# Two of the four moves of each unit's turned probabilities go from SyncE to ScalarE

## The chip, the cores and the metric

One core of a Trainium2 chip runs the whole program. The metric is the device time of one execution in microseconds (us); lower is better. Two executions of the kernel before took 2779.14 and 2780.52 us, median 2779.83.

## What is computed

One layer of a sequence model on x of 2048 tokens by 2048 features, all in float32. The normalised input is multiplied with one wide weight matrix; its columns feed three head groups, each with its own gate; one output matrix follows. Cut to what matters here:

```python
h = rmsnorm(x, ln_gain)
q_a, k_a, v_a, g_a, b_c, c_c, x_c, g_c, q_m, g_m = split(h @ w_in)
# A: 16 query heads, 2 key heads of 64; a chunk of 64 queries sees 128 keys; bias, one sink a head
p = softmax(concat([q_a k_a^T / 8 + bias, sink]))[..., :-1];  o_a = p @ v_a
# M: 4 heads of 128 over 256 memory tokens
p = softmax(q_m k_m^T / sqrt(128));                           o_m = p @ v_m
o_c = b_c * causal_dwconv3(c_c * x_c)
out = x + concat([silu(g_a) o_a, silu(g_c) o_c, silu(g_m) o_m]) @ w_out
```

## The kernel before

The program is written out by hand for each engine; every engine runs its own instructions strictly in the order of the text, and waits for others on semaphores. PE is the matmul engine, DVE VectorE, ACT ScalarE, POOL GpSimd, SP SyncE.

**Slots.** All work is set against slots. A slot is one load of 512 KB of weights: SP loads it (`weights`, L540), ACT rounds its two halves into w_hi (`high`, L765, two instructions), POOL computes w_lo = raw - w_hi (L655), and PE multiplies three products for each pair of parts (hi hi, hi lo, lo hi), 24 products of 512 columns a slot (L1729 to L1731). ACT and POOL prepare slot s + 2 in iteration s. After 16 slots for the memory tokens come four groups of 512 tokens with 52 slots each (blocks KV, QA0, QA1, QM, C, X, B), and then 224 slots for gates and output (L1801 to L1805), in which no attention is left.

**Units.** In each group 24 units of attention run beside the slots: A units (one chunk of queries and one key head) in the odd slots 17 to 47, M units (memory attention) in the even slots 34 to 48. So there is one unit in two slots at first, and one in each slot from 33 on. For a unit in slot s:

- PE computes the scores behind the matmuls of slot s (`scores`, L1872 or L1866).
- DVE adds the bias (L1421), finds the maxima (L1433, or L1411 for M), and ACT computes the exponentials (`softmax_exp`, four instructions L984 for A, two L975 for M, with sums).
- DVE divides (L1449) and transposes blocks of 32 by 32 into blocks_t (`turn_probs`, L1458); this raises the semaphore turned.
- Four DMAs of 64 KB (`move_probs`, L548) bring the four groups of 32 rows of blocks_t to probs_t, all of them issued by SP. SP does this before the weights of slot s + 6; its wait for turned stands ahead of them.
- In iteration s + 2, for an A unit, ACT writes pt_hi from probs_t (`probs_high`, L995) when all four moves have landed, and DVE pt_lo (L1381). DVE does this before it touches the next A unit's scores.
- In iteration s + 3 PE multiplies with the values (`values`, L1900 and L1901, or L1891 for M), ACT copies the result (`attention_out`, L1010 for A, L1005 for M), and for A DVE adds the second half (`attention_sum`, L1393), which comes ahead of DVE's softmax in that iteration. PE's next `values` waits for it.

**ACT's order in iteration s** is: parts of the next group's input (L891), `evacuate`, `high` for slot s + 2, `attention_out`, `probs_high`, `softmax_exp`, then the issues of larger transfers where the tables name the slot: t_store and t_load (weight sums), rows_store, h_store (L808), x_load (L776), and x_square and x_scale on xt (L795, L801), and h_load (L814). An ACT DMA that waits on a semaphore stands in the same order as ACT's arithmetic.

Of the kernel before, what the change touches and what calls it, by code (L numbers as in the profile page):

```python
# [80 lines left out]
UNITS = len(UNIT)  # L81
# [4 lines left out]
SCORES_AT = {s: u for u, s in enumerate(UNIT_SLOTS)}  # L86
# [100 lines left out]
def program(nc, x, mem, ln_gain, w_in, q_norm_a, k_norm_a, sinks, conv_w, mem_ln_gain, w_mem_kv,  # L187
# [5 lines left out]
    with ctx:  # L193
        def sb(name, shape, dt=F32):
            return ctx.enter_context(nc.sbuf_tensor(name, shape, dt))
# [4 lines left out]
        def sem(name):  # L200
            return ctx.enter_context(nc.semaphore(name))
# [48 lines left out]
        blocks_t = sb("blocks_t", [P, 2, 4, P])  # L250
        probs_t = sb("probs_t", [P, 2, 4, P])
# [103 lines left out]
        turned = sem("turned")  # L355
        moved = [sem(f"moved{i}") for i in range(2)]
# [178 lines left out]
        def _(sp):  # L535
# [7 lines left out]
            def move_probs(g, u):  # L543


                sp.wait_ge(turned, g * UNITS + u + 3)
                for i in range(4):
                    sp.dma_start(probs_t[:, u % 2, i, :], blocks_t[32 * i:32 * i + 32, u % 2, :, :]  # L548
                                 ).then_inc(moved[u % 2], 16)

# [71 lines left out]
            for j in range(OUT_SLOTS):  # L622
                r, i, s = j // PAIR_SLOTS, j % PAIR_SLOTS // PRODUCT_SLOTS, j % PRODUCT_SLOTS
# [124 lines left out]
        def _(act):  # L748
# [95 lines left out]
            def low_load(kq):  # L844

                act.wait_ge(half_used, 2 * OUT_BASE - 16 + 4 * kq + 4)
                h_fetch(1, kq, tiles4(x_low, kq), low_in[kq])
# [39 lines left out]
            def h_high(g, k):  # L887

                act.wait_ge(h_in[k // 4], 16 * g + 16)
                act.wait_ge(half_used, 2 * (MEM_SLOTS + (g + 1) * GROUP_SLOTS - SB_SLOTS) + k + 1)  # L890
                nc.scalar.activation(in_32s(h_hi[:, k, :]), x_row(h_buffer(k // 4), k),  # L891
                                     ACT.Copy).then_inc(x_hi, 1)
# [25 lines left out]
            def t_store(g, n):  # L918

                act.wait_ge(t_step, 4 * (SB_SLOTS * g + n + 1))  # L920
                act.dma_start(w_sums[g, :, P * n:P * n + P, :].rearrange("s p c -> p s c"),
                              stage[:, :, :]).then_inc(t_stored, 16)
# [39 lines left out]
            def conv_latest_tap(g):  # L962

                for b in range(4):
                    act.wait_ge(bank_free[b], g * USES + MEM_USES + 6)
                    nc.scalar.activation(ungated[:, 8 + b, :], early[:, 8 + b, :], ACT.Copy,
                                         scale=taps[:, 2, b:b + 1]).then_inc(conv_first, 1)

            def softmax_exp(g, u):
                U = g * UNITS + u  # L970
                if UNIT[u][0] == "M":
                    act.wait_ge(shifted, U + 1)
                    act.wait_ge(turned, U + 1)
                    for h in range(2):
                        e = nc.scalar.activation(probs[:, u % 2, 256 * h:256 * h + 256],  # L975
                                                 ps_t[:, 256 * h:256 * h + 256], ACT.Exp,
                                                 bias=shift[:, h:h + 1],
                                                 accum_out=total[:, h:h + 1])
                else:
                    act.wait_ge(sink_ready, g * LOCAL_UNITS + LOCAL[u] + 1)  # L980
                    nc.scalar.activation(sink_exp[:, :], sink_in[:, :], ACT.Exp)
                    for p in range(4):
                        s = probs[:, u % 2, P * p:P * p + P]
                        e = nc.scalar.activation(s, s, ACT.Exp, bias=shift[:, p:p + 1],  # L984
                                                 accum_out=total[:, p:p + 1])
                e.then_inc(exped, 1)

            def probs_high(g, u):
                U = g * UNITS + u
                act.wait_ge(moved[u % 2], g * 768 + (u // 2) * 64 + 64)  # L990
                if LOCAL[u]:
                    act.wait_ge(valued, g * UNITS + LOCAL.index(LOCAL[u] - 1) + 2)
                else:
                    act.wait_ge(valued, g * UNITS + 1)
                nc.scalar.activation(pt_hi[:, :], probs_t[:, u % 2, :, :].rearrange("p a q -> p (a q)"),  # L995
                                     ACT.Copy).then_inc(pt_high, 1)
# [59 lines left out]
            def a_high(j, h):  # L1056

                r, i, s = j // PAIR_SLOTS, j % PAIR_SLOTS // PRODUCT_SLOTS, j % PRODUCT_SLOTS
                name = PRODUCTS[i][0]
                kq = (2 * s + h) // 4  # L1060
                if name in ("S3", "S1", "S4"):
                    act.wait_ge(s_made, sums_to(j) - 1 + h)
                elif name == "S2":
                    act.wait_ge(s2_step, 16 * (r // 2) + 4 * s + h + 3)
                elif gating(r):
                    if name == "A22":
                        act.wait_ge(low_in[2 + kq], 16 * (r // 4) + 16)
                    else:
                        act.wait_ge(top_in[kq + 2 * (name == "A12")], 16 * (r // 4) + 16)
                elif name == "A11":  # L1070
                    act.wait_ge(mixed, 32 * (r // 4) + 16)
                else:
                    act.wait_ge(mixed, 32 * (r // 4) + 32)
                if j >= 2:
                    act.wait_ge(half_used, 2 * (OUT_BASE + j - 2) + h + 1)
                else:
                    act.wait_ge(t_stored, 16 * SB_SLOTS * GROUPS)
                if j in (2, 3):
                    act.wait_ge(o_ready, GROUPS * UNITS + 1)
                nc.scalar.activation(in_32s(a_parts(j, h)[0]), a_source(j, h),  # L1080
                                     ACT.Copy).then_inc(a_hi_ready, 1)

            for g in range(GROUPS):
                base = g * GROUP_SLOTS + MEM_SLOTS
                last = g == GROUPS - 1
                for s in range(GROUP_SLOTS):
                    if last and s >= GROUP_SLOTS - 2:
                        for h in range(2):
                            a_high(s - GROUP_SLOTS + 2, h)
                    if g:  # L1090
                        for k in H_SPLIT_NEXT.get(s, ()):
                            h_high(g - 1, k)
                    if not last:
                        for k in H_SPLIT_AT.get(s, ()):
                            h_high(g, k)
                    if s in LAST_SLOT:
                        evacuate(*LAST_SLOT[s], g, base + s + 1)
                    if s == CONV_FIRST_AT:
                        conv_latest_tap(g)
                    high((s + 2) % 4, base + s + 2)  # L1100
                    if s in VALUES_AT:
                        attention_out(g, VALUES_AT[s])
                    if s in SPLIT_AT:
                        probs_high(g, SPLIT_AT[s])
                    if s in SCORES_AT:
                        softmax_exp(g, SCORES_AT[s])
                    if s in T_STORE_AT:
                        t_store(g, T_STORE_AT[s])
                    if s in T_LOAD_AT:
                        t_load(g, T_LOAD_AT[s])  # L1110
                    if s in ROWS_STORE_AT:
                        rows_store(g, ROWS_STORE_AT[s])
                    if g:
                        for quarter in ROWS_STORE_NEXT.get(s, ()):
                            rows_store(g - 1, quarter)
                    if s in H_STORE_AT:
                        h_store(g, H_STORE_AT[s])
                    if s in X_LOAD_AT:
                        x_load(g, X_LOAD_AT[s])
                    if s in X_SQUARE_AT:  # L1120
                        x_square(g, X_SQUARE_AT[s])
                    if s in X_SCALE_AT:
                        x_scale_of(g, X_SCALE_AT[s])
                    if last:
                        for kq in TOP_LOAD_AT.get(s, ()):
                            top_load(kq)
                        if s in LOW_LOAD_AT:
                            low_load(LOW_LOAD_AT[s])
                    else:
                        for kq in H_LOAD_AT.get(s, ()):  # L1130
                            h_load(g, kq)
# [871 lines left out]
```

## Time and profile before

| | |
|---|---|
| median of 2 executions | 2779.83 us |
| profiled execution | 2779.99 us, its span 2778.2 us |
| PE, DVE, ACT, POOL busy | 95%, 67%, 45%, 63% of the span |
| granted clock of PE over the span | 0.98 |
| moves (64 KB each) | 384, median 2.2 us from issue to landing |
| four groups of tokens | up to about 1500 us; gates and output behind |

A busy share of PE of 95% is a mean over stages; matmuls are pipelined, and what a stage is bounded by is read from its waits. SPq and ACTq are the issues of DMAs by SP and ACT, which don't count as busy. A line of the timeline gives start, duration, engine, line, operation and tiles, and in brackets how long the engine was idle before it and what ended that.

### The profile page before, as it was taken

To read this page: it belongs to the slowest core of one execution; us is meant where nothing else is said; L and a number is where in the kernel's file an instruction comes from. 1 tells how busy PE (TensorE), PEld (TensorE's weight loads), DVE (VectorE), ACT (ScalarE), POOL (GpSimd) and SP (SyncE) were. 2 spreads that over 40 slices of the span, in tenths; PEclk is the share of its full clock that TensorE was granted. 3 is DMA by queue.
4 is the path that set the end of the run, shared out by engine and by line. 5 is a ranking of instruction groups with operands and counts; after the bars stand their busy time and mean duration, and the time that the engine had idled before them with its cause. 6 is when DMAs were issued, how large, how long until landed. Compare 5 with 4: busy or idle time off the path is not lost.

```text
span 2778.2 us, 33924 instructions
## 1 busy us (share of the span) xinstructions
PE 2631.3 (95%) x12092; PEld 2151.6 (77%) x12092; DVE 1855.8 (67%) x2324; ACT 1258.1 (45%) x2660; POOL 1741.5 (63%) x1190
## 2 busy tenths in 40 slices
PE   7999899998999989999899999999999999999999
PEld 6877678776777768777687778777888878877887
DVE  4347576376764666646666786887677786797667
ACT  6344353454443545434453445443444444443443
POOL 6577444775547755387554567766667567666766
PEclk9999999999999999999999999999999999999999
DMA  8566756666556666656668633247445633324444
GB/s 252 157 202 188 232 151 200 226 201 203 171 183 225 198 183 197 203 186 217 179 203 258 222 92 96 87 141 223 152 144 167 219 91 99 91 91 144 159 129 144
DMA packets 329613, 479.70 MB, mean 173 GB/s; under 512 B 19094, under 2 KB 135908, under 8 KB 326884
## 3 DMA queue, kind: packets, MB, share of 16 engines
q1 hardware_dynamic: 191412, 278.28, 33.7%
q10 hardware_dynamic: 138032, 199.25, 21.6%
q8 instruction: 97, 1.59, 0.2%
q14 instruction: 72, 0.59, 0.1%
HBM read 355.03 MB, written 84.67 MB: 158 GB/s over the span
## 4 chain that ended last, share of the span: by engine, by line
PE 52%; DVE 20%; issue 8%; ACT 7%; POOL 5%; DMA 4%; SPq 3%; ACTq 1%; DVEq 0%; POOLq 0%
PE acc L1729 6%; PE acc L1730 6%; PE acc L1731 6%; PE acc L1801 5%; PE acc L1803 5%; PE acc L1805 5%; POOL w_lo L655 3%; DMA probs_t<-blocks_t 3%; DVE a_lo L1592 3%; SPq L548 2%; DVE blocks_t L1458 2%; ACT probs L984 2%; PE ps_s L1801 2%; DVE s_sum L1587 2%; PE ps_o L1801 1%
## 5 line engine op out<-in xcount | busy, mean ns | idle before, releaser
L655 POOL TENSOR_TENSOR w_lo<-raw,w_hi 128x512 fp32r<-128x512 f32 x896 | 1307.8, 1475 | 949.1 <-ACT w_hi L765 947.2
L765 ACT ACTIVATE w_hi<-raw 128x512 fp32r<-128x512 f32 x896 | 544.5, 627 | 808.7 <-PE acc L1731 267.0
L1729 PE MATMUL acc<-w_hi,h_hi 128*128 128x512 f32 (+1 forms) x1024 | 377.9, 369 | 12.6 <-POOL w_lo L655 12.5
L1731 PE MATMUL acc<-w_hi,h_lo 128*128 128x512 f32 (+1 forms) x1024 | 372.9, 364 | 0.0
L1730 PE MATMUL acc<-w_lo,h_hi 128*128 128x512 f32 (+1 forms) x1024 | 372.7, 364 | 0.0
L1729 PE MATMUL acc<-h_hi,w_hi 128*128 128x512 f32 x768 | 319.6, 416 | 7.8 <-DVE early L1507 5.7
L1730 PE MATMUL acc<-h_lo,w_hi 128*128 128x512 f32 x768 | 306.1, 399 | 0.0
L1731 PE MATMUL acc<-h_hi,w_lo 128*128 128x512 f32 x768 | 305.6, 398 | 0.0
L1592 DVE TENSOR_TENSOR a_lo<-s_sum,a_hi 128x512 fp32r<-128x512 f32 x192 | 216.9, 1162 | 33.8 <-ACT a_hi L1080 29.5
L1729 PEld LDWEIGHTS acc<-w_hi,h_hi 128*128 128x128 f32 x1024 | 194.1, 190 | 52.8 <-POOL w_lo L655 21.2
L1731 PEld LDWEIGHTS acc<-w_hi,h_lo 128*128 128x128 f32 x1024 | 193.9, 189 | 30.8
L1730 PEld LDWEIGHTS acc<-w_lo,h_hi 128*128 128x128 f32 x1024 | 194.2, 190 | 28.8
L1080 ACT ACTIVATE a_hi<-s_sum 128x512 fp32r<-128x512 f32 x192 | 117.7, 629 | 172.1 <-DVE s_sum L1587 167.1
L1729 PEld LDWEIGHTS acc<-h_hi,w_hi 128*128 128x128 f32 x768 | 149.6, 195 | 45.6 <-POOL w_lo L655 9.0
L1801 PE MATMUL acc<-a_hi,w_hi 128*128 128x512 f32 x448 | 176.3, 394 | 7.8 <-issue 4.2
L1801 PE MATMUL acc<-w_hi,a_hi 128*128 128x512 f32 x448 | 175.0, 391 | 4.6 <-DVE a_lo L1592 4.4
L1803 PE MATMUL acc<-a_lo,w_hi 128*128 128x512 f32 x448 | 175.6, 392 | 0.0
L1805 PE MATMUL acc<-a_hi,w_lo 128*128 128x512 f32 x448 | 175.5, 392 | 0.0
L1803 PE MATMUL acc<-w_lo,a_hi 128*128 128x512 f32 x448 | 174.3, 389 | 0.0
L1805 PE MATMUL acc<-w_hi,a_lo 128*128 128x512 f32 x448 | 174.3, 389 | 0.0
L1731 PEld LDWEIGHTS acc<-h_hi,w_lo 128*128 128x128 f32 x768 | 148.2, 193 | 33.1
L1730 PEld LDWEIGHTS acc<-h_lo,w_hi 128*128 128x128 f32 x768 | 149.0, 194 | 30.6
(278 smaller groups left out, 5456.0 us busy)
## 6 DMA issues: line engine op xcount, KB each, us to landing
raw<-in_w_in SPq DMA_DIRECT2D x256, 512.0 KB, 4.3
raw<-w_sums SPq DMA_DIRECT2D x128, 512.0 KB, 3.7
w_sums<-stage ACTq DMA_DIRECT2D x32, 1024.0 KB, 5.4
probs_t<-blocks_t SPq DMA_DIRECT2D x384, 64.0 KB, 2.2
raw<-in_w_out SPq DMA_DIRECT2D x48, 512.0 KB, 3.6
early<-h_rows ACTq DMA_DIRECT2D x17, 1024.0 KB, 7.8
xt<-in_x ACTq DMA_DIRECT2D x16, 1024.0 KB, 8.6
stage<-in_w_in ACTq DMA_DIRECT2D x32, 512.0 KB, 4.7
```

The costliest lines, as they stand in the source:

```text
L548: sp.dma_start(probs_t[:, u % 2, i, :], blocks_t[32 * i:32 * i + 32, u % 2, :, :]).then_inc(moved[u % 2], 16)
L655: nc.gpsimd.tensor_tensor(w_lo[:, at, :], raw[:, slot_mod, HALF * half:HALF * half + HALF], w_hi[:, at, :].bitcast(F32), ALU.subtract).the ...
L765: nc.scalar.activation(w_hi[:, 2 * (slot_mod % 2) + half, :], raw[:, slot_mod, HALF * half:HALF * half + HALF], ACT.Copy).then_inc(hi_read ...
L984: e = nc.scalar.activation(s, s, ACT.Exp, bias=shift[:, p:p + 1], accum_out=total[:, p:p + 1])
L1080: nc.scalar.activation(in_32s(a_parts(j, h)[0]), a_source(j, h), ACT.Copy).then_inc(a_hi_ready, 1)
L1592: nc.vector.tensor_tensor(in_32s(lo), a_source(j, h), in_32s(hi.bitcast(F32)), ALU.subtract).then_inc(a_lo_ready, 1)
L1729: nc.tensor.matmul(dst, st[0], mv[0], start=first, stop=False)
L1730: nc.tensor.matmul(dst, st[0], mv[1], start=False, stop=False)
L1731: return nc.tensor.matmul(dst, st[1], mv[0], start=False, stop=last)
L1801: nc.tensor.matmul(banks[t][:, :], st[0], mv[0], start=first, stop=False, skip_group_check=True)
L1803: nc.tensor.matmul(banks[t][:, :], st[0], mv[1], start=False, stop=False, skip_group_check=True)
L1805: last = nc.tensor.matmul(banks[t][:, :], st[1], mv[0], start=False, stop=s == 3 and h == 1, skip_group_check=True)
```

## The change

SP issues moves 0 and 1 of each unit, at its place of before. ACT issues moves 2 and 3, directly behind the unit's exponentials in `softmax_exp`, ahead of all transfers and of x_square and x_scale of that iteration; before them it waits for turned, which DVE raises with the unit's transpose. The semaphores that the readers wait for are the same, with the same counts. It does so for all 96 units. Nothing is computed otherwise.

```diff
--- before.py
+++ after.py
@@ -544,7 +544,7 @@
 
 
                 sp.wait_ge(turned, g * UNITS + u + 3)
-                for i in range(4):
+                for i in range(2):
                     sp.dma_start(probs_t[:, u % 2, i, :], blocks_t[32 * i:32 * i + 32, u % 2, :, :]
                                  ).then_inc(moved[u % 2], 16)
 
@@ -985,6 +985,13 @@
                                                  accum_out=total[:, p:p + 1])
                 e.then_inc(exped, 1)
 
+            def move_probs(g, u):
+
+                act.wait_ge(turned, g * UNITS + u + 3)
+                for i in range(2, 4):
+                    act.dma_start(probs_t[:, u % 2, i, :], blocks_t[32 * i:32 * i + 32, u % 2, :, :]
+                                  ).then_inc(moved[u % 2], 16)
+
             def probs_high(g, u):
                 U = g * UNITS + u
                 act.wait_ge(moved[u % 2], g * 768 + (u // 2) * 64 + 64)
@@ -1104,6 +1111,7 @@
                         probs_high(g, SPLIT_AT[s])
                     if s in SCORES_AT:
                         softmax_exp(g, SCORES_AT[s])
+                        move_probs(g, SCORES_AT[s])
                     if s in T_STORE_AT:
                         t_store(g, T_STORE_AT[s])
                     if s in T_LOAD_AT:
```

## Rows read from the trace of the kernel before

**Rows 1.** The page: busy time by engine, and the chain that ended last

```profile
PE 2631.3 (95%) x12092; PEld 2151.6 (77%) x12092; DVE 1855.8 (67%) x2324; ACT 1258.1 (45%) x2660; POOL 1741.5 (63%) x1190
...
PE 52%; DVE 20%; issue 8%; ACT 7%; POOL 5%; DMA 4%; SPq 3%; ACTq 1%; DVEq 0%; POOLq 0%
```

**Rows 2.** Busy time by stretch: start:end, length, engines with instructions, clock, DMA, GB/s

```profile
640.00:800.00 160.00, 143.42 (x686) 117.00 (x687) 106.47 (x183) 73.06 (x214) 72.73 (x52) 0.95 0.64 189
```

**Rows 3.** Waits of the matmul engine, 430 to 780 us: total, times, longest

```profile
PE ps_o L1900 <- DVE pt_lo L1381: 14.0, 5, 5.4
PE ps_o L1891 <- DVE ungated L1393: 3.9, 3, 2.5
```

**Rows 4.** Timeline of ACT, 706 to 719 us: start, duration, instruction, idle before

```profile
706.81 0.39 ACT L984 ACTIVATE probs<-probs,shift 128x128 f32<-128x128 f32 x1
...
708.36 1.14 ACT L765 ACTIVATE w_hi<-raw 128x512 fp32r<-128x512 f32 x2
...
709.52 0.77 ACT L1010 ACTIVATE ungated<-ps_o 64x256 f32<-64x256 f32 x2
...
713.12 1.15 ACT L765 ACTIVATE w_hi<-raw 128x512 fp32r<-128x512 f32 x2
...
714.16 0.38 ACT L1005 ACTIVATE ungated<-ps_o 128x256 f32<-128x256 f32 x1
...
714.82 0.63 ACT L995 ACTIVATE pt_hi<-probs_t 128x512 fp32r<-128x512 f32 x1 [0.28 <-DMA probs_t<-blocks_t]
...
718.75 0.39 ACT L984 ACTIVATE probs<-probs,shift 128x128 f32<-128x128 f32 x1
```

**Rows 5.** Timeline of DVE, the same stretch

```profile
709.62 1.10 DVE L1458 STREAM_TRANSPOSE blocks_t<-probs 128x512 f32<-128x512 f32 x1
710.64 0.81 DVE L1393 SCALAR_TENSOR_TENSOR ungated<-ps_o,ungated 64x256 f32<-64x256 f32 x2
...
715.16 1.09 DVE L1458 STREAM_TRANSPOSE blocks_t<-probs 128x512 f32<-128x512 f32 x1
716.18 0.65 DVE L1381 TENSOR_TENSOR pt_lo<-probs_t,pt_hi 128x512 fp32r<-128x512 f32 x1
```

**Rows 6.** The moves' line: issue min/median/max ns, first and last start; landing

```profile
L548 SPq DMA_DIRECT2D probs_t<-blocks_t x384: 544/603/2455, 188.1 to 1487.7; - x192
...
DMA to landing us min/median/max: 2.1/2.2/6.8
```

**Rows 7.** Waits of the whole span, all engines

```profile
ACT pt_hi L995 <- DMA probs_t<-blocks_t: 98.9, 35, 7.7
...
DVE ungated L1393 <- ACT ungated L1010: 16.0, 11, 2.3
```

**Rows 8.** Timeline of ACT, 589 to 595 us: issues behind a wait

```profile
589.75 3.32 ACTq L808 DMA_DIRECT2D h_rows<-early  x4
...
593.83 1.15 ACT L765 ACTIVATE w_hi<-raw 128x512 fp32r<-128x512 f32 x2 [6.85 <-issue]
```

**Rows 9.** Timeline of ACT, slot 35: the second h_load's issue

```profile
676.09 3.48 ACTq L814 DMA_DIRECT2D xt<-h_rows  x1
```

**Rows 10.** The chain of waits, 676 to 690 us: the landing of slot 35's moves

```profile
681.28 6.79 DMA probs_t<-blocks_t
```

**Rows 11.** Timelines of ACT and DVE at slots 43 and 44

```profile
734.40 2.55 ACT L966 ACTIVATE ungated<-early,vecs 128x512 f32<-128x512 f32 x4
...
738.82 0.85 DVE L1393 SCALAR_TENSOR_TENSOR ungated<-ps_o,ungated 64x256 f32<-64x256 f32 x2 [2.06 <-ACT ungated L1010]
```

**Rows 12.** Timeline of DVE behind slot 45's transpose

```profile
751.45 2.98 DVE L1291 TENSOR_TENSOR h_lo<-early,h_hi 128x512 fp32r<-128x512 f32 x2
```

**Rows 13.** Timeline of ACT at slots 28 and 29

```profile
615.71 2.01 ACT L801 ACTIVATE xt<-xt,x_scale 128x2048 f32<-128x2048 f32 x1
...
620.24 0.63 ACT L995 ACTIVATE pt_hi<-probs_t 128x512 fp32r<-128x512 f32 x1 [1.48 <-DMA probs_t<-blocks_t]
```

**Rows 14.** Timeline of SP at slot 37's place: move_queries

```profile
644.09 8.61 SPq L555 DMA_DIRECT2D early<-ungated  x4
```

## The prediction

> **What bounds the kernel now.** I read the page's busy line and the chain that ended last [rows 1]. The matmul engine is busy 95% of the span and makes 52% of the chain; DVE has 20%, ACT 7%, transfers 4%, SP's issue 3%. So the end is mostly the matmuls' own time, but not everywhere. The table by stretch [rows 2] shows 640 to 800 us, the second half of group 1's softmax work, with the matmul row 143.4 us busy of 160 at a granted clock of 0.95. The moves' issues are spread from 188.1 to 1487.7 us [rows 6], so the change can act only before 1500.
>
> Then the waits of the matmul engine in group 1 (430 to 780 us) [rows 3]: 14.0 us for pt_lo and 3.9 us for the sum L1393, the two largest there. So in this stage the softmax loop and the matmuls are nearly level: when the loop is late, the matmuls wait for it in values().
>
> Last the loop itself, at the pair of units (slots 39 and 40) where it runs without disturbance. One A and one M unit take from A's first exponential at 706.81 to the next A's at 718.75, 11.9 us. ACT [rows 4]: **two w_hi at 708.36, in the instant in which A's exponentials end, attention_out at 709.52**, two w_hi behind M's exponentials at 713.12, M's output at 714.16, pt_hi at 714.82. DVE [rows 5]: A's transpose 709.62 to 710.72, **the sum L1393 directly behind it at 710.64**, M's transpose 715.16 to 716.25, **pt_lo directly behind it at 716.18**. DVE does not pause except for ACT's exponentials. What the reader is to see: while DVE divides and transposes (2.3 us for A: from the exponentials' end, 0.09 behind 708.36, to 710.72), ACT does the work that DVE wants next. Matmuls: one slot is 24 products; two slots with their scores and values fill about the same 12 us.
>
> **What the change removes.** SP issues two moves instead of four. Four take 2.49 us, 0.60 each, and the last lands 2.2 us after its issue [rows 6]. Two on each of two queues: both pairs are issued in 1.2 us, so the last lands 1.2 us earlier. That is worth something only where pt_hi waits for the landing: 98.9 us in 35 of 64 units [rows 7], so at most 35 x 1.2 = 42 us over the kernel. SP's weights behind it also go out 1.2 us earlier; what they wait for is POOL's low parts, and the matmuls' large waits are elsewhere [rows 3]: nothing.
>
> The Trainium skill ("DMA: Bandwidth & Descriptors", section "Issuing engines are not separate DMA queues") says that starting transfers from several engines saves only the sequencer's time to start them, and calls it small. By that rule alone the sum would be the gain of this paragraph and no more; it says nothing of what the new issuer leaves undone.
>
> **What it adds.** ACT's queue is in order. Behind each of 96 units' exponentials it will stand until the transpose is done (2.3 us in the A unit of [rows 4, 5]) and then issues two moves. ACT's issue of a like transfer is not in the trace; the nearest are its four h_store issues, 3.32 us [rows 8], 0.83 each, with contention, and SP's 0.60 each. I take 1.2 us for two, and 1.7 as the other end. The same rows are the proof that a wait ahead of an issue holds ACT: h_store's issues wait for DVE's x_gain until 589.75, and the w_hi behind them comes only at 593.83, after 6.85 us in which ACT does nothing. So per unit ACT gives away 2.3 + 1.2 = 3.5 us in which it now works; all of it on the end would be 96 x 3.5 = 336 us.
>
> Replay of the pair, counted from each transpose's end (T):
> A unit: 1.2 issue + 1.14 w_hi + 0.77 attention_out = 3.1 us, then the sum, which now starts at T - 0.08. **+3.2 us.**
> M unit: 1.2 + 1.15 + 0.38 + 0.63 = 3.35 us to pt_hi's end, then pt_lo, which now starts at T. **+3.3 us.** The pt_hi there is that of the A unit before, whose moves have landed by then.
> Together +6.5 on 11.9 us, and nothing covers it, as DVE has no pause and the matmuls are level with it.
>
> The other seven pairs of a group, by the same counting:
> Slot 33: the second half also waits for block C's four copies, now behind M's transpose: +3.2 + 4.5, say +8.
> Slot 35: h_load's issues, 3.48 us for the second alone, lie beside the exponentials and DVE's division now [rows 9] and come behind the moves then: A's sum +4.9, M's half +2.6, +7.5. Here the moves themselves gain: unit 35's took 6.79 us to land behind that 2 MB [rows 10] and will be ahead of it; but ACT would by then be the later one.
> Slots 37 and 41: M's half is partly covered (a slow landing, DVE's additions for block X): +4.4 each.
> Slot 43: ACT's 2.55 us of L966 already makes DVE's sum wait 2.06 us [rows 11]; behind the transpose it makes it wait 5.7: +3.6, and +3.3 for M: +7.
> Slots 45 and 47: DVE has its own work behind each transpose, 2.98 us of h_lo behind A's [rows 12] and the convolution behind M's. That hides most: A +1.9, M +0.3, +2.2 each.
> Sum 8 + 7.5 + 4.4 + 6.5 + 4.4 + 7 + 2.2 + 2.2 = 42 us a group.
>
> Slots 17 to 31 (A units only, two slots apart): ACT has longer until pt_hi. At 615.71 it does 2.01 us of x_scale, w_hi at 617.62, and waits 1.48 us for the landing before pt_hi at 620.24 [rows 13]. Then: T at 616.12 + 1.2 + 1.14 + 0.77 + 2.0 + 1.14 = 622.4, +2.1. Without x_scale about 0. At slot 25 ACT has an x_square and the copies of a whole block between the exponentials and pt_hi, with no pause, so all 3.5 us count. At slot 31 SP's moves stand behind move_queries, 8.61 us of issue beside ACT's h_store, until 652.74, 6.5 us after T [rows 14]; with h_store held back that issue runs faster: -3. The eight: 0.3 + 1.5 + 0.1 + 1.2 + 3.5 + 2.1 + 1 - 3 = +6.7, say +6 a group.
>
> So +48 a group, x4 = 192; the last group has one top_load instead of two at slot 35, -3. **+189 us.** The profiled execution took 2779.99 us (span 2778.2), the median of the runs shown is 2779.83, so they are one number here. 2780 + 189 = 2969; I say **2967**. The clock: in the stretch in which the matmuls wait for the loop it is 0.95 [rows 2]. More waits will bring more time at the lower level, but beside a late loop a slower matmul costs nothing; zero, and some tens of us at the upper end.
>
> **Rivals.**
> A, gain: ACT's delayed work is short enough, and the earlier landing decides. The place is pt_hi L995, the price -1.2 us in each of 35 units, 2738 us. For it: the 98.9 us of rows 7. It decides where ACT's work between transpose and pt_hi is under the landing's 2.2 us. Against it: that work is 1.14 + 0.77 + 1.14 us or more [rows 13]. 5%.
> B, hidden: ACT is busy only 45% [rows 1], so 3.5 us find room there. 2780. Against: its pauses are those in which DVE computes for it, and what ACT does before them is what DVE waits for. 8%.
> C, half: of the two delays of a pair only one reaches the next pair, because the matmuls' slack of a slot or DVE's other work takes the other. 3.3 x 8 x 4 = 106 us, 2886. 15%.
> D, all of it: every unit pays 3.5 us, and the half clock comes more often when matmuls wait at each unit, 3116 us or near it. 7%.
> My own case: 65%.
>
> **The numbers.** A measurement of this kernel tells 2% (56 us) from no change. Faster by over 2% needs 2724, below even rival A, so only 2% for more gain than I can find. Within 2%: the rest of A and B, 11%. Slower: C, D and my case, 87%. The range: my terms are uncertain by a third (issue at 1.7 us for two adds 96 x 0.5 = 48 at most, covered halves take away as much), 2905 to 3040; to take in C it starts at 2865. **2865 to 3045.**
>
> **What the profile after would show.** ACT's time from the end of an A unit's exponentials to the next w_hi grows from nothing to about 3.5 us. The waits "DVE ungated L1393 <- ACT ungated L1010" (16.0 us in 11 now [rows 7]) grow to some 100 us or more, and pt_lo's wait for pt_hi grows; pt_hi's wait for the moves falls from 98.9 us to under 40. The matmul engine's waits for pt_lo and L1393 grow from 18 to about 60 us a group. The distance between A units' exponentials in slots 39 and 41 is 18 us. From 1500 us on (counted back from the end) nothing changes. I would be wrong if w_hi came right behind the exponentials, if the sum came at the transpose's end, or if the matmuls' waits of a group did not grow.

## The result and the profile after

The changed kernel took 3071.52 us (two executions, 3071.40 and 3071.63) against 2779.83: ratio 1.105 (95% interval 1.103 to 1.108), **292 us slower**. The direction and the main mechanism (ACT is held until the transpose is done) were those of the prediction; the size was not: 187 us were forecast, and the time lies above the range, which ended at 3045.

The page of the changed kernel, its lines that answer to [rows 1]:

```profile
PE 2724.4 (89%) x12092; PEld 2217.0 (72%) x12092; DVE 1865.5 (61%) x2324; ACT 1259.1 (41%) x2660; POOL 1709.5 (56%) x1190
...
PE 43%; DVE 22%; ACT 12%; issue 9%; ACTq 8%; POOL 5%; DMA 1%; SPq 0%; DVEq 0%; POOLq 0%
```

The matmul engine's share of the chain went from 52% to 43%; ACT's from 7% to 12%, and ACT's queue, where the issues are, from 1% to 8%.

The busy time by stretch of group 1, slots 17 to 33 and slots 33 to 48 (columns as in [rows 2]):

```profile
612.80:752.50 139.70, 114.24 (x485) 89.32 (x484) 80.37 (x121) 56.63 (x143) 71.89 (x49) 0.91 0.55 165
752.50:917.00 164.50, 119.38 (x506) 95.04 (x505) 76.53 (x131) 57.05 (x173) 54.36 (x42) 0.86 0.45 130
```

Before, these stretches took 119.7 and 112.4 us (from the first exponential of slot 17's unit to that of slot 33's, and on to slot 48's); now they take 139.7 and 164.5. Busy times of DVE and ACT stay what they were (76.5 and 57.1 us in the second stretch), the matmul engine is busy for only 119.4 of the 164.5 us, and its granted clock falls from 0.99 to 0.86.

The waits of the matmul engine in group 1 (answer to [rows 3]; 502 to 923 us, which lies to group 1's units as 430 to 780 us does before):

```profile
PE ps_o L1899 <- DVE ungated L1401: 29.4, 7, 5.4
PE acc L1737 <- POOL w_lo L655: 16.7, 9, 4.4
PE acc L1737 <- ACT ungated L959: 10.3, 1, 10.3
PE ps_o L1908 <- DVE pt_lo L1389: 8.5, 7, 3.2
```

The 14.0 and 3.9 us for pt_lo and the sum are 8.5 and 29.4 now, and 16.7 us for POOL's low parts and 10.3 us for ACT's copies of block C have come beside them.

ACT at slots 39 and 40 (answer to [rows 4]):

```profile
820.33 0.39 ACT L984 ACTIVATE probs<-probs,shift 128x128 f32<-128x128 f32 x1
...
824.70 1.47 ACTq L992 DMA_DIRECT2D probs_t<-blocks_t  x2
...
826.27 1.15 ACT L765 ACTIVATE w_hi<-raw 128x512 fp32r<-128x512 f32 x2 [4.30 <-PE acc L1739]
...
827.44 0.77 ACT L1017 ACTIVATE ungated<-ps_o 64x256 f32<-64x256 f32 x2
...
833.75 1.47 ACTq L992 DMA_DIRECT2D probs_t<-blocks_t  x2
835.32 1.16 ACT L765 ACTIVATE w_hi<-raw 128x512 fp32r<-128x512 f32 x2 [4.45 <-issue]
836.38 0.37 ACT L1012 ACTIVATE ungated<-ps_o 128x256 f32<-128x256 f32 x1
836.64 0.62 ACT L1002 ACTIVATE pt_hi<-probs_t 128x512 fp32r<-128x512 f32 x1
...
841.04 0.39 ACT L984 ACTIVATE probs<-probs,shift 128x128 f32<-128x128 f32 x1
```

and DVE there (answer to [rows 5]):

```profile
823.59 1.08 DVE L1466 STREAM_TRANSPOSE blocks_t<-probs 128x512 f32<-128x512 f32 x1
828.25 0.85 DVE L1401 SCALAR_TENSOR_TENSOR ungated<-ps_o,ungated 64x256 f32<-64x256 f32 x2 [3.58 <-ACT ungated L1017]
...
832.62 1.10 DVE L1466 STREAM_TRANSPOSE blocks_t<-probs 128x512 f32<-128x512 f32 x1
837.29 1.82 DVE L1389 TENSOR_TENSOR pt_lo<-probs_t,pt_hi 128x512 fp32r<-128x512 f32 x1 [3.58 <-ACT pt_hi L1002]
```

The A unit's transpose ends at 824.67. ACT's two moves are issued from 824.70 to 826.17, w_hi follows, attention_out begins at 827.44, and the sum L1401 begins at 828.25, 3.58 us behind the transpose where it was directly behind it. With M's transpose the same: it ends at 833.72, pt_hi begins at 836.64 and pt_lo at 837.29. The next A unit's exponentials start at 841.04: 20.7 us for the pair, before 11.9.

The waits of the whole span (answer to [rows 7]), and ACT's new line, its issue times and the time to landing (answer to [rows 6]):

```profile
ACT w_hi L765 <- issue: 284.9, 62, 8.4
DVE ungated L1401 <- ACT ungated L1017: 225.4, 60, 8.1
DVE pt_lo L1389 <- ACT pt_hi L1002: 197.0, 56, 7.7
```

```profile
L992 ACTq DMA_DIRECT2D probs_t<-blocks_t x192: 551/633/1514, 187.2 to 1776.6; - x192
...
DMA to landing us min/median/max: 2.1/2.4/6.1
```

The sum's waits for ACT grew from 16.0 to 225.4 us, pt_lo's waits for pt_hi from 154.3 to 197.0. No wait of pt_hi for the moves, 98.9 us before, is left: the moves land in time now, but ACT itself comes later than they do. Behind the last unit nothing changed: from the first exponential of slot 48 in the last group to the end are 1296 us before and 1297 after.

### The profile page after: what moved, and what is told of

Read it like the earlier page. It is cut to its first block, busy times and chain, and to the rows that moved or that the text cites. A ratio compares the mean times of both kernels' runs of the same rounds, so it can differ in the third digit from the quotient of the medians.

```text
span 3069.8 us, 33924 instructions
## 1 busy us (share of the span) xinstructions
PE 2724.4 (89%) x12092; PEld 2217.0 (72%) x12092; DVE 1865.5 (61%) x2324; ACT 1259.1 (41%) x2660; POOL 1709.5 (56%) x1190
## 4 chain that ended last, share of the span: by engine, by line
PE 43%; DVE 22%; ACT 12%; issue 9%; ACTq 8%; POOL 5%; DMA 1%; SPq 0%; DVEq 0%; POOLq 0%
PE acc L1809 5%; PE acc L1811 5%; PE acc L1813 5%; PE acc L1737 4%; ACTq L992 4%; PE acc L1738 4%; PE acc L1739 4%; ACT w_hi L765 3%; DVE blocks_t L1466 3%; POOL w_lo L655 3%; ACT probs L984 2%; DVE probs L1457 2%; DVE a_lo L1600 2%; PE ps_s L1809 1%; DVE probs L1429 1%
## 5 line engine op out<-in xcount | busy, mean ns | idle before, releaser
L655 POOL TENSOR_TENSOR w_lo<-raw,w_hi 128x512 fp32r<-128x512 f32 x896 | 1282.1, 1447 | 1255.3 <-ACT w_hi L765 1253.4
L1737 PE MATMUL acc<-h_hi,w_hi 128*128 128x512 f32 x768 | 341.0, 444 | 92.7 <-ACT ungated L959 39.7
L1738 PE MATMUL acc<-w_lo,h_hi 128*128 128x512 f32 (+1 forms) x1024 | 379.4, 371 | 0.0
L1738 PE MATMUL acc<-h_lo,w_hi 128*128 128x512 f32 x768 | 323.5, 421 | 0.0
L1739 PE MATMUL acc<-h_hi,w_lo 128*128 128x512 f32 x768 | 320.6, 417 | 0.0
L1737 PEld LDWEIGHTS acc<-h_hi,w_hi 128*128 128x128 f32 x768 | 161.3, 210 | 138.9 <-issue 69.6
L1389 DVE TENSOR_TENSOR pt_lo<-probs_t,pt_hi 128x512 fp32r<-128x512 f32 x64 | 77.3, 1208 | 197.0 <-ACT pt_hi L1002 197.0
L1401 DVE SCALAR_TENSOR_TENSOR ungated<-ps_o,ungated 64x256 f32<-64x256 f32 x128 | 53.4, 417 | 226.4 <-ACT ungated L1017 225.4
L1739 PEld LDWEIGHTS acc<-h_hi,w_lo 128*128 128x128 f32 x768 | 158.7, 207 | 37.5
L1738 PEld LDWEIGHTS acc<-h_lo,w_hi 128*128 128x128 f32 x768 | 161.0, 210 | 33.8
```

What stands on the lines that cost most here:

```text
L655: nc.gpsimd.tensor_tensor(w_lo[:, at, :], raw[:, slot_mod, HALF * half:HALF * half + HALF], w_hi[:, at, :].bitcast(F32), ALU.subtract).the ...
L1737: nc.tensor.matmul(dst, st[0], mv[0], start=first, stop=False)
L1738: nc.tensor.matmul(dst, st[0], mv[1], start=False, stop=False)
L1739: return nc.tensor.matmul(dst, st[1], mv[0], start=False, stop=last)
```

## The experiments

All run beside the kernel before, whose median beside them was 2777 to 2779 us. Gains and losses are against that median. The edits are shortened. Those of experiments 2, 10, 14 and 15 start from the kernel before, the others are shown against the changed kernel. H, Q and W are three theories of the loss, explained in the first expectation. "A group" is one of the four groups of tokens; the stretch of slots 17 to 33 took 120 us before and 139 in the changed kernel, that of 33 to 48 111 (105 in the last group) and 165 (160).

**1. The wait alone.**

```diff
 def move_probs(g, u):            # ACT; SP issues all four
     act.wait_ge(turned, g * UNITS + u + 3)
-    for i in range(2, 4): act.dma_start(...)
```

> ACT waits for turned behind each unit's exponentials but issues nothing; SP issues all four moves as before. Theory H (ACT is held: its w_hi, attention_out and pt_hi come only behind the transpose, and DVE's loop waits for them): in the tight pair the sum starts 1.14 + 0.77 = 1.9 us behind the transpose instead of 3.6 and pt_lo 2.2 instead of 3.6, so a bit over half of the loss of 292 us: 2920 to 2960 us. Theory Q (issuing transfers on ACT, or two queues beside each other, is what costs): 2780. Theory W (the loss is w_hi that comes too late for POOL and the matmuls): w_hi comes right behind the transpose, 1.5 us earlier than in the changed kernel; about 2900.

2952.23 us, ratio 1.063 (1.061 to 1.065): +175, 60% of the loss with not one move issued by ACT. The sum waited for ACT:

```profile
DVE ungated L1398 <- ACT ungated L1014: 130.5, 53, 5.4
```

Theory Q cannot have this.

**2. The issues alone.**

```diff
+    for i in range(2, 4):        # no wait ahead; source a constant tile, target a spare array
+        act.dma_start(spare[...], mem_k[32 * i:32 * i + 32, 0:2, :]).then_inc(spared, 16)
```

> The kernel before, and ACT issues two transfers of 64 KB behind each unit's exponentials with no wait ahead of them (from a constant tile in SBUF to a spare array in HBM, results unused); SP issues all four moves. 192 more transfers than before. H: ACT's sequencer hands them out while the exponentials run, so 1.5 us of issue are mostly covered: 2780 to 2830. Q: most of the loss, over 3000.

2786.19 us, ratio 1.0033 (1.0021 to 1.0045): +9. Issues cost little where nothing holds them: ACT's queue hands them out while the exponentials run. In slot 39 they start at 707.72 and 708.09 us, the exponentials run from 707.80 to 709.34, and w_hi starts there. Two issues behind the wait cost 292 - 175 = 117 us, 1.2 us for each of 96 units. These are not quite the same issues: here the target is memory, and they took 0.33 and 0.44 us. Experiment 4 makes the comparison with the very same moves.

**3. All four by ACT.**

```diff
-    for i in range(2, 4):        # ACT
+    for i in range(4):           # ACT; SP none
```

> ACT issues all four moves behind its wait, SP none. Two more issues of 0.74 us each stand ahead of w_hi: H: each of 96 units pays another 1.5 us on the loop, +140, and the last move lands 1.2 to 1.5 us later than in the changed kernel but still ahead of pt_hi: 3190 to 3240 us. Q: the queues no longer work beside each other, no change or a gain against 3072. W: +0 to +100.

3161.11 us, ratio 1.138 (1.136 to 1.140): 90 us more than with two, 0.93 us a unit where I expected 1.5, and below the range of 3190 to 3240. Two more issues delay w_hi by 1.1 us (it starts 2.70 us behind the transpose's end in slot 39, with two moves 1.60), so the third and fourth take 0.53 each. The sum:

```profile
DVE ungated L1401 <- ACT ungated L1017: 284.7, 60, 8.2
```

**4. The same moves, one iteration later.**

```diff
 probs_high(g, SPLIT_AT[s])
+move_probs(g, SCORES_AT[s - 1])  # ACT: the unit of the slot before
 softmax_exp(g, SCORES_AT[s])
-move_probs(g, SCORES_AT[s])
```

> The same two moves of each unit by ACT, with the same wait, but one iteration later: behind that iteration's w_hi, attention_out and pt_hi and ahead of its exponentials. By then the transpose is done and ACT would be idle, waiting for DVE's shift. H: the whole loss goes, and the earlier landing is left: 2740 to 2785 us. Q: the same issues and queues, so about 3070. W: w_hi is on time, so also 2780; it differs from H in that nothing is gained or lost at DVE's sum.

2789.66 us, ratio 1.0040 (1.0025 to 1.0055). Same queues, same 192 issues, same wait: 280 of the 292 us are gone. It is 5 us above the range of 2740 to 2785, since the expected gain did not come. The sum and pt_hi:

```profile
DVE ungated L1402 <- ACT ungated L1017: 12.9, 11, 2.1
...
ACT pt_hi L1002 <- DMA probs_t<-blocks_t: 10.6, 9, 3.2
```

pt_hi's wait for the moves fell from 98.9 to 10.6 us and yet the kernel is not faster: slots 17 to 33 took 124 us, 4 more than before. There the issues, 1.5 us, stand ahead of the next iteration's x_scale and w_hi, and thereby of pt_hi.

**5 and 6. Only the A units, only the M units.**

```diff
-for i in range(2):               # SP
+for i in range(2 if UNIT[u][0] == "A" else 4):    # e5; "M" in e6; ACT likewise
```

> Only the 64 A units are as in the changed kernel; SP issues all four moves of the 32 M units. H (ACT is held, and the delays of A and M units add, each at its own place, A's at the sum L1393, M's at pt_lo): the tight pair takes 11.9 + 3.6 = 15.5 us, slots 17 to 33 stay at 139 us as in the changed kernel, 33 to 48 at 138; a group loses 46 of 72 us: 2960 us. Theory C (of two delays in a pair only one reaches the next pair): near 3070.

> Only the 32 M units are as in the changed kernel. H: slots 17 to 33 as before (120 us), the tight pair 11.9 + 3.6 + 1.2 (pt_lo beside POOL's w_lo) = 16.7 us, 33 to 48 at 140 us; a group loses 28 us: 2890 us. The losses of this run and of the run with A units alone add up to the 292 us of the changed kernel. C: this run alone near 3070 in slots 33 to 48, and the two sum to much more than the whole.

A units alone: 2962.67 us, +184 (ratio 1.066, 1.064 to 1.068). M units alone: 2872.96, +95 (1.034, 1.032 to 1.036), 17 us less than expected. Together 279 of 292: the two delays of a pair add. With M units alone slots 17 to 33 stayed at 120 us and 33 to 48 took 134; rival C is out.

**7. The other issues ahead of the wait.**

```diff
 softmax_exp(g, SCORES_AT[s])
-move_probs(g, SCORES_AT[s])
 t_store, t_load, rows_store
+move_probs(g, SCORES_AT[s])
```

> As the changed kernel, but the issues of t_store, t_load and rows_store of an iteration stand ahead of ACT's wait, where they go out while the exponentials run. They are 0.4 to 1.1 us each in 13 of 24 units. H: what stood behind the moves no longer delays w_hi and what follows: up to 0.7 us in 13 x 4 units, 3072 - 35 = 3035 us. If those issues were covered anyway: 3072.

3026.83 us, ratio 1.090 (1.088 to 1.091): 45 us come back; in group 1 it is 5.6 us in slots 17 to 33 and 4.6 in 33 to 48. Transfers that were issued beside the exponentials had been pushed behind the wait too, a part of the loss that I had counted only at slot 35.

**8. Four chosen slots.**

```diff
+ACT_MOVES = (21, 31, 35, 37)     # in the place of experiment 4; SP issues four elsewhere
```

> ACT issues two moves only for the units in slots 21, 31, 35 and 37, at the place ahead of the next iteration's exponentials; SP issues all four of the others. In the run with that place for all units the distances behind slots 21, 31, 35 and 37 shrank by 1.9, 1.5, 0.5 and 3.0 us in group 1, while those behind 17, 23, 25, 27, 39 and 41 grew by 0.9 to 2.3. H (at that place a unit gains where the landing releases pt_hi and loses where ACT has work before pt_hi): 4 x 6.9 = 28 us less than before, about 2750. If gain and loss are given back at the next unit: 2777.

2769.78 us, ratio 0.9966 (0.9954 to 0.9977): 8 us less than before, not 28. In group 1 slot 21 won 1.8 us and slot 23 gave back 1.4, slot 37 won 3.0 and slot 39 gave back 2.0; slot 31's 2.5 stayed.

**9 and 10. Fewer matmuls in the loop's slots.**

```diff
 matmul(dst, st[0], mv[0]); matmul(dst, st[0], mv[1])
-matmul(dst, st[1], mv[0])        # left out in slots 34 to 48
```

A third of the products of these slots is missing, so the output is not that of the layer.

> The changed kernel, and the third product of each pair of parts is left out in slots 34 to 48 of each group (120 of 360 products of 512 columns in those slots; part of the computation is missing). That takes 120 x 0.23 = 27 us of matmuls a group at the full clock. H (the loop of ACT and DVE alone sets the time of slots 33 to 48, and the half clock of the waiting matmul engine costs nothing): 165 us of these slots stay over 158, the whole 3045 to 3072. Theory K (the extra loss over my replay is the matmul engine at half its clock): they fall by 12 us a group or more, the whole below 3020.

> The kernel before with the same third products left out in the same slots. It tells how level loop and matmuls were: H: the loop sets these slots here too, 110 us go to 104 to 110 a group, the whole 2750 to 2775. If the matmuls set them: 110 go to 90, the whole 2700.

After with fewer: 3072.87 us, unchanged. Before with fewer: 2775.14, ratio 0.9987 (0.9978 to 0.9996): 4 us, though the matmul engine was busy for 72 us less (2558.9 instead of 2631.3). Slots 33 to 48 of group 1, by stretch: the changed kernel with fewer products, the kernel before, and that with fewer:

```profile
752.40:916.40 164.00, 102.21 (x397) 79.80 (x396) 76.35 (x131) 56.99 (x173) 54.05 (x42) 0.79 0.44 130
...
661.90:774.30 112.40, 105.74 (x513) 85.88 (x512) 76.55 (x131) 56.40 (x174) 58.30 (x42) 0.99 0.62 186
...
658.70:769.40 110.70, 88.46 (x401) 69.64 (x400) 76.96 (x131) 56.38 (x174) 57.89 (x42) 0.92 0.62 189
```

In the changed kernel the matmul engine is busy for 102.2 us instead of 119.4, at a granted clock of 0.79 instead of 0.86, and the stretch still takes 164.0 us. In the kernel before it is busy for 105.7 of 112.4 us, and with 88.5 instead the stretch takes 110.7. So in neither kernel do the products set the time of these slots, and then a slower clock does not cost time there either. "Nearly level" in my prediction was wrong for the kernel before: its matmuls follow the loop of ACT and DVE. That error did not lower the forecast: if the matmuls have slack, it is the loop's delay that shows in full.

**11. attention_out and pt_hi ahead of w_hi**, in the changed kernel.

```diff
-high((s + 2) % 4, base + s + 2)
 attention_out(g, VALUES_AT[s]); probs_high(g, SPLIT_AT[s])
+high((s + 2) % 4, base + s + 2)
```

> The changed kernel, but in each iteration ACT does attention_out and pt_hi ahead of the two w_hi. The wait and the issues stay. H (what counts is what ACT still has to do between the wait and the results that DVE wants): the sum starts 1.5 + 0.8 = 2.3 us behind the transpose instead of 3.6, pt_lo 2.3 instead of 3.6 and clear of POOL's w_lo, of which the replay lacked 1.2 us: 3.7 us of the 8.8 of the tight pair come back, 25 to 30 us a group: 2950 to 2970. W (w_hi late for POOL and matmuls): w_hi comes later still, so slower than 3072.

2984.24 us, ratio 1.074 (1.072 to 1.075): 87 us come back, 14 fewer than the weakest case of H, although w_hi is later still. So theory W is out. DVE at slots 37 and 38:

```profile
791.71 1.08 DVE L1466 STREAM_TRANSPOSE blocks_t<-probs 128x512 f32<-128x512 f32 x1
...
795.14 0.85 DVE L1401 SCALAR_TENSOR_TENSOR ungated<-ps_o,ungated 64x256 f32<-64x256 f32 x2 [2.35 <-ACT ungated L1017]
...
798.92 1.11 DVE L1466 STREAM_TRANSPOSE blocks_t<-probs 128x512 f32<-128x512 f32 x1
...
802.51 0.69 DVE L1389 TENSOR_TENSOR pt_lo<-probs_t,pt_hi 128x512 fp32r<-128x512 f32 x1 [2.48 <-ACT pt_hi L1002]
```

The sum comes 2.35 us behind the transpose; pt_lo comes 2.5 us behind it and lasts 0.69 us. In the changed kernel it lasts 1.82 in the tight pair. POOL's timeline there:

```profile
836.03 2.54 POOL L655 TENSOR_TENSOR w_lo<-raw,w_hi 128x512 fp32r<-128x512 f32 x2 [3.99 <-ACT w_hi L765]
```

The line holds two instructions. ACT writes w_hi just before pt_hi, so the second of the two w_lo starts at 837.28, 0.01 us ahead of DVE's pt_lo (837.29 to 839.11). With w_hi last POOL has a pause there, and the mean of the 64 pt_lo falls from 1208 to 808 ns (824 before the change). To lie beside each other is not enough: in [rows 5] pt_lo starts at 716.18, beside a w_lo that ends at 716.28 and 0.06 us ahead of the next; it takes 0.65 us, and that next w_lo takes 1.75 instead of 1.27. In both kernels all pt_lo of over 1 us (7 before, 28 after) start with 0.7 us or more of a w_lo still to run; none of the other 93 has more than 0.31 us ahead of it. So pt_lo finishes about half a microsecond behind the w_lo under which it starts. That the order of start decides is read from these traces; no run changed it alone.

**12. Slot 31 alone.**

> ACT issues two moves only for the unit in slot 31, ahead of the next iteration's exponentials. With slots 21, 31, 35 and 37 so treated the distance behind slot 31 fell by 2.5 us a group (19.7 to 17.2), while what 21 and 37 won (1.9 and 2.9) was given back behind slots 23 and 39. H: 4 x 2.5 = 10 us less than before, the same as with the four slots: 2768.

2766.53 us, ratio 0.9958 (0.9945 to 0.9970): 13 us less than before, the lowest median of all, with an interval that overlaps that of experiment 8. SP there:

```profile
638.12 4.25 SPq L556 DMA_DIRECT2D early<-ungated  x4
642.41 3.15 SPq L549 DMA_DIRECT2D probs_t<-blocks_t  x2
```

move_queries is issued in 4.25 us instead of the 8.61 of [rows 14], and the moves 2.2 us behind the transpose's end, before 6.5. That h_store is held back behind ACT's two issues, and so leaves the queries' transfers free, is the likely cause of the shorter issue; it was not tried apart from the moves.

**13 and 14. The sum behind DVE's other work**, slots 17 to 29.

```diff
-attention_sum(g, VALUES_AT[s])           # first in DVE's iteration
 ... query means, scale, turns, flips, gain
+attention_sum(g, VALUES_AT[s])           # where s <= 32
```

> The changed kernel; for the A units in slots 17 to 29 DVE does the sum L1393 behind its other work of that iteration (scale and turns of the queries, flips and gain of x) instead of ahead of it. H (that work stands behind a late sum and makes pt_lo late): at slot 21 pt_lo comes 3.3 us earlier, at 29 2.8 us, elsewhere ACT's pt_hi is the later one: slots 17 to 33 fall from 139 to 133 us, the whole to 3048. Theory A (ACT alone): 139 us stay, 3072.

> The control: the same place of the sum in the kernel before. There the sum is not late, so its place is worth nothing: slots 17 to 33 stay at 120 us, the whole 2772 to 2786, by H and by A.

In the changed kernel 3056.78 us, ratio 1.1006 (1.0989 to 1.1023), 15 us less where 24 were expected; in the kernel before 2778.94, ratio 1.0002 (0.9992 to 1.0012). The distances behind slots 21 and 29 fell from 17.2 to 12.5 us and from 20.0 to 17.2; before they were 13.1 and 17.2. That behind slot 27 grew by 1.9, though pt_lo starts 11.05 us behind the exponentials as without the edit. The difference is in two small DVE instructions behind it (L1444 and L1447), which take 1.00 and 1.20 us instead of 0.16 each while POOL is at subtractions. So the late sum is part of the growth in slots 17 to 33 (5.4 of 20.0 us in group 1); the rest follows ACT, with the issues of experiment 7 and such meetings with POOL among it.

**15 and 16. w_hi last in the kernel before, and with slot 31.**

> The kernel before with attention_out and pt_hi ahead of the two w_hi in each iteration. H: 1.15 us less where ACT's own work holds pt_hi (slots 17, 23, 25) and pt_lo is clear of POOL's w_lo, so 3 to 6 us a group: 2755 to 2770. W (w_hi must not be late): slower than 2779.

> ACT issues two moves for the unit in slot 31 alone, and attention_out and pt_hi stand ahead of the two w_hi. H: the two gains touch other slots and add: 12.9 us of slot 31 and what the order of w_hi gives in the kernel before: 2742 to 2760. If that order is worth nothing: 2767.

2781.80 us, ratio 1.0016 (1.0004 to 1.0028), and 2772.50, ratio 0.9978 (0.9968 to 0.9987), 6 us behind slot 31 alone (the two intervals just touch). Both expectations failed: what orders ACT better once it has been held is worth nothing, or a little less, where it is not held.

## Why the prediction was right in kind and wrong in size

**Right.** The term that decides, ACT held until the transpose's end, was named with its place. In the tight pair 2.3 us of wait was forecast and 2.7 measured (821.97, where the exponentials end, to 824.67); the sum +3.2 (measured +3.7), pt_lo +3.3 (+3.6), the distance between the A units 18 us (20.7), and w_hi came 4.3 us behind the exponentials where 3.5 were forecast. Experiments 1, 4 and 5 with 6 show it, and that the earlier landing is worth nothing as long as ACT is the later one. Of the marks, the sum's wait for ACT, pt_hi's wait for the moves and the unchanged part behind the last unit held. One did not: the matmul engine's waits for pt_lo and the sum were to grow to 60 us in group 1 and are 37.9; another 27.0 stand at POOL's low parts and ACT's copies, which hang on the same late ACT. Rival A (gain), B (hidden) and C (half) fell. D (every unit pays 3.5 us, and the half clock, 3116 us) comes nearer in number, 44 us off against 105 for my case, but not in kind: the distances behind slots 19, 23, 27 and 31 grew by 0.9 to 1.3 us, and experiments 9 and 10 leave the clock nothing. The rule from the Trainium skill, "Issuing engines are not separate DMA queues" in "DMA: Bandwidth & Descriptors", is borne out as far as it goes: with the issues on two engines and ACT not held nothing was gained (experiment 4, ratio 1.0040), and issues added to ACT by themselves made 9 us of difference.

**Wrong: the size of the terms.** The distances in group 1 from one A unit's exponentials to the next A unit's (in the last column from slot 47 to 48), growth forecast and measured:

```
slot      17   19   21   23   25   27   29    31    sum   33   35   37   39   41   43   45   47   sum
forecast  0.3  1.5  0.1  1.2  3.5  2.1  1.0  -3.0   6.7   8.0  7.5  4.4  6.5  4.4  7.0  2.2  2.2  42
measured  4.2  0.9  4.1  1.3  4.7  0.9  2.8   1.1  20.0   8.5  9.2  5.3  8.8  6.0 10.0  2.7  1.8  52
```

72 us a group instead of 48, times four 288, of 292 measured. The step of the prediction that failed most is that for slots 17 to 31: "The eight: ... say +6 a group". It came to 20.0 us in group 1. Three things were left out of it:

1. For slot 21 I asked only when pt_hi could come ("without x_scale about 0"). DVE's timeline there in the changed kernel:

```profile
649.96 1.08 DVE L1466 STREAM_TRANSPOSE blocks_t<-probs 128x512 f32<-128x512 f32 x1
654.50 0.85 DVE L1401 SCALAR_TENSOR_TENSOR ungated<-ps_o,ungated 64x256 f32<-64x256 f32 x2 [3.45 <-ACT ungated L1017]
655.37 2.65 DVE L1368 TENSOR_TENSOR early<-early,q_scale 128x2048 f32<-128x2048 f32 x1
657.95 1.09 DVE L1284 STREAM_TRANSPOSE early<-xt 128x512 f32<-128x512 f32 x1
658.97 0.76 DVE L1389 TENSOR_TENSOR pt_lo<-probs_t,pt_hi 128x512 fp32r<-128x512 f32 x1
```

The sum, 3.45 us late, stands first in that iteration, and 3.6 us of DVE's own work behind it; pt_lo comes at 658.97, 3.4 us after pt_hi's start (655.55). DVE has one queue too, and a delay at its head passes through all that stands behind. Experiments 13 and 14 show it for slots 21 and 29.

2. At slot 17 ACT works from w_hi to pt_hi through an x_square and a block's copies with pauses of only 1.4 us in all, so that nearly its whole hold counts, as at slot 25; I had seen it at 25 alone. w_hi came 5.2 us later behind the exponentials, pt_hi 3.4, and pt_lo took 1.66 us instead of 0.84: 4.2. Of the hold 1.10 us are two issues of t_load. The issues of t_store, t_load and rows_store had moved behind the wait as well, which experiment 7 prices at 45 us in all.

3. At slot 31 the gain of 3 us was counted on h_store going out later. SP's part came true: move_queries took 4.10 us instead of 8.61, and the moves were issued 2.1 us behind the transpose. But pt_hi then hung on ACT, where t_store's issue now took 1.48 us behind the moves and the four of h_store 7.8 us behind that, with the w_hi and pt_hi of the next iteration last. Experiment 7 has t_store's issue at 0.37 us beside the exponentials, those of h_store at 5.7, and the distance at 17.4 instead of 20.8.

In slots 33 to 48 the sum was short by 10 us, a fifth of the measured 52; single slots differed by -0.4 to +3.0. Two issues behind the wait take 1.47 us, not 1.2 (1.7 was about as far off on the other side): an estimate of 15 x 0.27 = 4 us. pt_lo meets POOL's w_lo in the five pairs from slot 35 to 43 and lasts 1.80 to 1.82 us there instead of 0.65 to 0.69, 5.7 us in all, of which the replay had nothing. The issues of t_store, t_load and rows_store are worth 4.6 us (experiment 7). Together that is more than the missing 10, so part of it is covered; the runs don't say which. I had let the range's lower side take in rivals that the rows spoke against, and its upper side only the issue's price; it should have held covers that fail.

## What to carry to other kernels

Before a transfer is put on an engine that computes, ask what that engine still has to do between the wait and the result that others want of it; that, and not the price of the issue, is the cost (175 us for the bare wait, 9 us for two bare issues a unit). The same two transfers cost 12 us instead of 292 when they stood behind what others wanted of the engine, one iteration later. And a delay is to be followed through every queue that it enters, with the whole of what stands behind the late instruction, up to the loop's end.

## What the runs showed of the chip that was not expected

Two of the same issues take 1.47 us on ACT's queue and 1.20 on SP's in the changed kernel, and four on ACT 2.55 us. A DVE subtraction of 128 x 512 that starts just after a POOL subtraction of the same shape lasts 1.8 us instead of 0.65 to 0.69; where DVE started 0.06 us ahead, it was POOL's that took longer, 1.75 instead of 1.27. And a third of the products could leave 15 slots of each group with no change in time (3072.87 against 3071.52 us), though the page of the changed kernel counts the matmul engine as busy for 89% of the span; in the kernel before, at 95%, it was worth 4 us.
